# Attention projections of three head pairs as seven block products, interleaved with the retention projections

## The reference, cut to what matters

```python
h = rms_norm(x, norm1_g)
proj = h @ w_in            # 2048 x 7168: retention q, k, v, gate and attention q, k, v, 8 heads of 128 each
ret = silu(rg) * head_group_norm(retention(rotary(rq), rotary(rk), rv))
att = chunk_attention(rms_norm(aq), rms_norm(ak), av, rel_bias)
x = x + concat(ret, att) @ w_out
h = rms_norm(x, norm2_g)
x = x + square(relu(h @ w_ff1)) @ w_ff2
```

## Time and profile before

| | |
|---|---|
| median of three runs | 1105.76 us |
| the profiled execution's own time | 1104.85 us |
| its span, first to last instruction | 1103.1 us |
| granted TensorE clock | 1.000 of full speed |
| TensorE busy | 1097.7 us, 5190 records |
| VectorE busy | 857.8 us |
| ScalarE busy | 695.4 us |
| GpSimd busy | 53.4 us |
| moved by DMA | 263.81 MB, mean 239 GB/s |

### The profile page before, as it was taken

One profiled execution on the slowest core, in us unless ns is written; L12 is line 12 of the kernel. 1 busy time (PEld: TensorE's weight loads), 2 busy tenths in 40 slices (PEclk: granted clock), 3 DMA queues, 4 the chain that ended last, 5 costly groups with the idle time before them and its releaser, 6 DMA issues.

```text
span 1103.1 us, 13129 instructions
## 1 busy us (share of the span) xinstructions
PE 1097.7 (100%) x5190; PEld 932.3 (85%) x5190; DVE 857.8 (78%) x803; ACT 695.4 (63%) x827; POOL 53.4 (5%) x69
## 2 busy tenths in 40 slices
PE   9999999999999999999999999999999999999998
PEld 9789989989988888888888888888888888888887
DVE  7876876866866678869778879778869787869784
ACT  6964664674674555777655677655677655577662
POOL 0100100100100000000000000000000000000000
DMA  9975774775776647878788787797787787787792
GB/s 360 306 255 173 206 254 170 198 263 173 191 277 217 242 178 198 263 264 239 226 297 229 252 282 218 233 299 221 254 284 214 243 290 222 261 277 221 245 279 93
DMA packets 43965, 263.81 MB, mean 239 GB/s; under 512 B 4864, under 2 KB 7680, under 8 KB 16256
## 3 DMA queue, kind: packets, MB, share of 16 engines
q1 hardware_dynamic: 37712, 220.61, 53.7%
q0 software_dynamic: 5760, 41.95, 20.3%
q10 hardware_dynamic: 432, 0.41, 0.1%
HBM read 260.85 MB, written 2.10 MB: 238 GB/s over the span
## 4 chain that ended last, share of the span: by engine, by line
PE 95%; ACT 0%; DVE 0%; issue 0%; DVEq 0%
PE acc L931 10%; PE acc L927 10%; PE acc L929 10%; PE acc L797 7%; PE acc L810 7%; PE acc L804 7%; PE bankC L889 4%; PE acc L889 4%; PE bankC L882 4%; PE acc L882 4%; PE acc L884 4%; PE bankC L884 4%; PE acc L624 2%; PE acc L629 2%; PE acc L636 2%; PE bankD L889 1%
## 5 line engine op out<-in xcount | busy, mean ns | idle before, releaser
L1779 DVE TENSOR_TENSOR w_lo<-raw,w_hi 128x2048 fp32r<-128x2048 f32 x180 | 410.8, 2288 | 126.8 <-ACT w_hi L1300 126.5
L1300 ACT ACTIVATE w_hi<-raw 128x2048 fp32r<-128x2048 f32 x180 | 344.7, 1916 | 220.0 <-PE acc L931 146.6
L1497 DVE TENSOR_TENSOR w_lo<-raw,w_hi 128x1024 fp32r<-128x1024 f32 (+1 forms) x150 | 164.9, 1110 | 47.5 <-ACT w_hi L1053 47.4
L1053 ACT ACTIVATE w_hi<-raw 128x1024 fp32r<-128x1024 f32 (+1 forms) x150 | 140.6, 965 | 21.6 <-DVE raw L1506 12.6
L797 PE MATMUL acc<-w_hi,hT_hi 128*128 128x384 f32 (+1 forms) x408 | 104.3, 374 | 0.1
L927 PE MATMUL acc<-w_hi,hF_hi 128*128 128x512 f32 x256 | 100.8, 394 | 0.0
L931 PE MATMUL acc<-w_hi,hF_lo 128*128 128x512 f32 x256 | 99.7, 390 | 0.0
L929 PE MATMUL acc<-w_lo,hF_hi 128*128 128x512 f32 x256 | 99.6, 389 | 0.0
L804 PE MATMUL acc<-w_hi,hT_lo 128*128 128x384 f32 (+1 forms) x408 | 97.7, 357 | 0.0
L810 PE MATMUL acc<-w_lo,hT_hi 128*128 128x384 f32 (+1 forms) x408 | 97.2, 356 | 0.0
L927 PE MATMUL acc<-w_hi,dF_hi 128*128 128x512 f32 x248 | 96.9, 391 | 0.0
(11 more groups left out here) (276 smaller groups left out, 1798.9 us busy)
## 6 DMA issues: line engine op xcount, KB each, us to landing
raw<-in_w_up SPq DMA_DIRECT2D x64, 1024.0 KB, 6.5
raw<-in_w_down SPq DMA_DIRECT2D x64, 1024.0 KB, 6.5
raw<-in_w_ret SPq DMA_DIRECT2D x32, 1024.0 KB, 5.7
raw<-in_w_att SPq DMA_DIRECT2D x28, 768.0 KB, 4.5
raw<-in_w_out SPq DMA_DIRECT2D x16, 1024.0 KB, 4.8
raw<-in_w_up POOLq DMA_DIRECT2D x16, 1024.0 KB, 8.8
raw<-in_w_down POOLq DMA_DIRECT2D x16, 1024.0 KB, 9.1
raw<-in_w_ret POOLq DMA_DIRECT2D x8, 1024.0 KB, 9.0
```

Of the source, the lines that this page charges most:

```text
L1053: nc.scalar.activation(piece(w_hi, q, 0, n), raw[:, r, half * n:(half + 1) * n], ACT.Copy).then_inc(hi_done, 1)
L1300: nc.scalar.activation(w_hi[:, ring(s)], raw[:, r, :], ACT.Copy).then_inc(slab_hi, 1)
L1497: nc.vector.tensor_tensor(piece(w_lo, q, 0, n), raw[:, IN_PLAN[i, READ_AT.get(step, step)][0], half * n:(half + 1) * n], piece(w_hi, q, 0, ...
L1779: nc.vector.tensor_tensor(w_lo[:, ring(s)], raw[:, r, :], w_hi[:, ring(s)].bitcast(f32), ALU.subtract).then_inc(slab_lo, 1)
```

## The change

In pairs 1 to 3 the attention projection too is done as seven block products over the first half of the depth, and as plain steps I2, I3, J2, J3 over the second half. The new products carry small letters: q1, p5, p6, p7, p3, q2, p4, each 12 matmuls of 384 columns, with slabs A, B, D, E. The order of the steps alternates: the products of the attention of pair i stand between the steps of the retention of pair i - 1, and its slab steps between the retention products of pair i. Pair 0 keeps its attention steps; its retention's Z and H steps fall into the next block. The lists are now one, `IN_ORDER`, of 85 steps instead of 76. The tables of `at_piece` are written anew on all engines; products are numbered n (0 for the retention of pair 0, odd n for attention, even n for retention). Retention uses the banks A and B for all heads but head 6.

```diff
+IN_ORDER = [(0, step) for step in "I0 J0 I1 J1 I2 Q1 J2 P5 I3 P6 J3 P7 P3".split()]
+IN_LOADS = [(0, name) for name in "I0 J0 I1 J1 I2 a J2 b I3 d J3".split()]
+IN_STARTS = [0]
+for _i in range(1, BLOCKS + 1):
+    _r, _here = "Z1 Q2 Z2 P4 H1 H2", "Z1 Q2 q1 Z2 P4 p5 H1 p6 H2 p7 p3 I2 q2 Q1 I3 p4 P5 J2 P6 J3 P7 P3"
+    _loads = "Z1 e A Z2 B D H1 H2 I2 E a I3 b d J2 J3" if _i < BLOCKS else "Z1 e Z2 H1 H2"
...
         def ret_banks(u):
-            return (bankA, bankB) if u % 2 else (bankC, bankD)
+            return (bankC, bankD) if u == HEADS - 2 else (bankA, bankB)
...
-                if step == "I0" and i:
-                    pe.wait_ge(acc_read_act, 8 * i - 3 + m)
-                elif step == "J0" and i:
-                    pe.wait_ge(acc_read_act, 8 * i - 1 + m)
-                elif step == "Q1" and i:
-                    pe.wait_ge(r_mix_lo, 2 * i - 1)
-                elif step == "P5":
+                n, up = in_pair(i, step), step.upper()
+                if up == "Q1" and n:
+                    pe.wait_ge(y_set, n)
+                    pe.wait_ge(w_set, n)
+                elif up == "P5":
...
-                        fresh = step in ("I0", "J0", "Q1", "P5") and t == 0
-                        wide = N if fresh else n
+                        fresh = step.upper() in ("I0", "J0", "Q1", "P5") and t == 0
+                        wide = N if fresh and i == 0 else n
...
             def ret_proj(u):
                 i, step = u // 2, "HZ"[u % 2 == 0] + "2"
-                if u % 2:
+                if u:
                     act.wait_ge(r_y, u)
                     act.wait_ge(r_gate_ok, u)
...
+            for i in range(1, BLOCKS):
+                add_b(2 * i - 1)
+                add_e(2 * i - 1)
+                ret_power(2 * i - 2)
+                mask_bias(i)
+                add_b(2 * i)
+                ret_power(2 * i - 1)
+                att_power(2 * i)
+                add_e(2 * i)
...
+                at_piece(i, 8, ret_proj, u)
+                at_piece(i, 9, ret_tanh, u)
+                at_piece(i, 12, keep_in_p5, n - 1)
+                at_piece(i, 13, ret_qT, u)
...
+                at_piece(i, 3, in_sum, n - 1, "b", "Q1")
+                at_piece(i, 9, ret_rotate, u)
+                at_piece(i, 11, ret_rotated, u)
+                at_piece(i, 11, in_sum, n - 1, "d", "P5")
+                at_piece(i, 13, ret_kT, u)
+                at_piece(i, 14, ret_decay, u)
...
+                at_piece(i, 26, ret_decay, u + 1)
+                at_piece(i, 26, in_sum, n, "b", "Q1")
+                at_piece(i, 28, ret_norm, u + 1)
+                at_piece(i, 31, in_sum, n, "d", "P5")
```

More of the change, by code:

```diff
@@ L508, in _ @@
             load_decay(1)
[L509 to L519, removed]
+            for i, name in IN_LOADS[11:]:
+                load_in(i, name)
+                if name == "D":
+                    load_bias(i)
+                elif name == "J3":
+                    load_decay(2 * i)
+                    load_decay(2 * i + 1)
             load_group(G_OUT, w_out, 0, N)
@@ L565, in ret_power, with add_second @@
                 nc.gpsimd.tensor_tensor(r_rs[:], r_ve[:], neg_half[:, 0:MT], ALU.pow).then_inc(r_rs_ok, 1)
-            def add_ret(i, into, c, k, done, count):
-                row = ((2 * i + c) * SLABS + k) * P
-                nc.gpsimd.dma_start(raw[:, IN_PLAN[i, into][0], :], w_ret[row:row + P, :],
+            def add_second(n, into, c, done):
+                table, cols = w_att if n % 2 else w_ret, SLAB_KT * pair_cols(n)
+                row = pair_row(n, c, 1)
+                nc.gpsimd.dma_start(raw[:, pair_raw(n, into)[0], 0:cols], table[row:row + P, :],
@@ L571, in add_ret, with add_b @@
                                     accum_op=ALU.add).then_inc(done, 16)
[L573 to L582, removed]
+            def add_b(n):
+                pool.wait_ge(in_summed, 2 * n + 1)
+                add_second(n, "b", 1, in_b)
@@ L624, in group @@
                             nc.tensor.matmul(acc[par][m][:, 0:n], hi[:, k, tile_cols(m)],
-                                             piece(w_hi, j, t * n, (t + 1) * n), start=j == 0 and t == 0, stop=False)
+                                             piece(w_hi, q, t * n, (t + 1) * n), start=j == 0 and t == 0, stop=False)
                     for m in range(MT):
@@ L713, in stationary @@
             def stationary(step, m, t):
+                step = step.upper()
                 if step in ("P5", "P6", "P7", "P3"):
@@ L846, in _ @@
                     f()
-            work = {j: work.get(8 * G_OUT + j, []) for j in range(PIECES)}
+            work = {j: work.get(IN_PIECES + j, []) for j in range(PIECES)}
             work[2] = work[2] + [lambda: pe.wait_ge(a_mix_lo, HEADS)]
@@ L1264, in _ @@
-            for q in range(8 * G_OUT):
+            at_piece(0, 12, keep_in_q1, 0)
+            at_piece(0, 16, keep_in_p5, 0)
+            at_piece(0, 18, att_proj, 0)
+            at_piece(0, 20, att_squares, 0)
+            at_piece(0, 22, att_proj, 1)
+            at_piece(0, 23, att_qT, 0)
+            at_piece(0, 24, set_y, 0)
+            at_piece(0, 25, set_h, 0)
+            at_piece(0, 25, att_squares, 1)
+            at_piece(0, 26, att_exp, 0)
+            at_piece(0, 27, att_pT, 0)
@@ new lines, in _ @@
+            i, u = BLOCKS, HEADS - 2
+            at_piece(i, 6, ret_proj, u)
+            at_piece(i, 8, ret_tanh, u)
+            at_piece(i, 9, ret_qT, u)
+            at_piece(i, 12, ret_proj, u + 1)
+            at_piece(i, 12, ret_scale, u)
+            at_piece(i, 13, ret_mix, u)
+            at_piece(i, 12, ret_tanh, u + 1)
+            at_piece(i, 13, ret_qT, u + 1)
+            at_piece(i, 16, ret_scale, u + 1)
+            at_piece(i, 17, ret_mix, u + 1)
+            for q in range(IN_PIECES):
@@ L1275, in _ @@
                     f()
-            group(G_OUT, N, N, {j: work.get(8 * G_OUT + j, []) for j in range(PIECES)})
+            group(G_OUT, N, N, {j: work.get(IN_PIECES + j, []) for j in range(PIECES)})
             def hi_slab(s):
@@ L1751, in _ @@
-            for q in range(8 * G_OUT):
+            at_piece(0, 10, in_sum, 0, "b", "Q1")
+            at_piece(0, 14, in_sum, 0, "d", "P5")
+            at_piece(0, 17, x_mean_squares)
+            at_piece(0, 19, set_z, 0)
+            at_piece(0, 19, s_lo, 2)
+            at_piece(0, 20, att_mean_squares, 0)
+            at_piece(0, 21, att_norm, 0)
+            at_piece(0, 23, set_w, 0)
+            at_piece(0, 25, att_bias_max, 0)
+            at_piece(0, 26, att_probs, 0)
+            at_piece(0, 27, att_mean_squares, 1)
```

450 lines of the change are left out of this document (233 added, 217 removed).

## The result

| | before | after |
|---|---|---|
| median | 1105.79 us (4 runs, 1105.53 to 1105.92) | 1116.76 us (4 runs, 1113.22 to 1118.08) |
| the profiled execution's own time, its span | 1104.85, 1103.1 us | 1118.08, 1115.9 us |
| granted clock | 1.000 | 0.995 |

The account below looks back on a forecast made before the run. TensorE's matmul pace bounds the projection stage: profiled 1104.85 - 6.9 removed + 3.3 waits at retention scores + 2.9 at J2 = 1104.15, against the median 1105.05; forecast 1105.0 us, 8-in-10 range 1100.8 to 1109.0.

Parts of the forecast that it names:

- What the change removes: TensorE, pairs 1 to 3: 36 matmuls of 384 columns fewer (6.3 us) and narrower openings (0.65 us), 6.9 us in all.
- the openings: Opening matmuls of I0 and J0, pairs 1 to 3: twelve 512-wide ones gone, 54 ns each, 0.65 us saved.
- place A: Retention scores of a pair's first head: TensorE waits for VectorE's key copy, 1.6 us in pairs 2 and 3, together 3.3.
- in pair 1 I get 0.15: Wait at pair 1's first-head retention scores: only 0.15 us, as probabilities come two pieces later and the evacuation isn't behind them.
- place B: Slab J2, pairs 1 to 3: its load lands late beside the accumulate into b; TensorE waits 1.0 us each, 2.9 in all.
- with 8.3: J2's load assumed to take 8.3 us, from an earlier 768 KB load beside an accumulate; high part then ends at 14.3.
- The bound of 9.5: Upper bound for J2's load: landing after 9.5 us, a wait of 2.1 us a pair.
- The lower bound of this term: J2's load lands in time (4.2 us), no wait for it; VectorE's backlog before J2's first low part still leaves about 0.4.
- What moved at no price: Bank reuse, last pair's retention, GpSimd's extra transfers and other short-release slabs such as H1: costed at nothing.
- late slabs make it slower: Rival, chance 0.23: J2 takes 9.5 us, H1 lands 1 us late, TensorE waits 9.3 in all; time 1111.5 us.
- beyond about 9 us: J2 load time above which late slabs make the kernel slower, where the waits pass 9.1 us.

Follow-up runs that it names:

- the kernel with all three edits: Changed kernel with accumulate into b behind the next ret_power, first head's scores one piece later, next pair's decay loads behind Z1's load: 1103.83 us, ratio 0.9983.
- the repaired kernels: Changed kernel with the accumulate into b later (1107.02 us); also with scores one piece later, with or without decay loads moved (1103.83 us each).
- the two other kernels with such waits: Changed kernel with scores one piece later: 1111.81 us; the kernel with all three edits plus J2's load held back by one slab: 1125.55 us.

## Why the prediction was wrong

By its own steps, with the profile's spans. The parts add up: the waits at J2 +8.5, at the scores +4.8, at the first pair's P6 +1.0; TensorE's low clock +4.1 (1096.2 us busy, 1092.1 in the kernel with the accumulate moved, which has the same instructions and full clock); the removed work -5.6 (1097.7 less 1092.1). Sum 12.8, the difference of the spans.

**What the change removes: 6.9 us forecast, 5.6 measured.** The count of 36 matmuls was right, and the openings hold. The shortfall is in the steady pairs: between the attention transposes of neighbouring pairs the kernel with all three edits has 82.5 us (126.89, 209.41, 291.86), of which 0.9 are waits, so 81.6; before it was 83.5. That is 1.9 us less a pair, not 2.3. What takes the other 0.4 is open. The rows at place A show that the first two matmuls of a step behind the scores take 0.43 us (90.98 to 91.41), the next two 0.35 (91.41 to 91.76), so each restart behind a small chain product has a price. But the new order does not have more of these: in the timelines of one pair (202.99 to 286.51 before, 209.41 to 291.86 in the kernel with all three edits) there are 16 in each.

**Place A: 3.3 us forecast, 4.8 measured.** Mechanism and size were right for pairs 2 and 3 (1.6 forecast, 1.55 and 1.57 measured). The failed step is "in pair 1 I get 0.15": it measured 1.69. I had started the ledger at the probabilities' transposes, where pair 1 is ahead by an evacuation. That lead is not there when it counts: r_qk is done 0.06 us ahead of its transposes in pair 1 and 0.22 in pair 2, and from there VectorE's 5.0 us against TensorE's 3.4 are alike in all pairs. The run with the scores later shows that the wait is real: moved by one piece, 3.2 us of it go and none comes back. (The terms printed in the prediction add up to 11.6 and 10.0 where it says 11.8 and 10.1, and at place B to 13.3 where it says 13.4; nothing turns on it.)

**Place B: 2.9 us forecast, 8.5 measured.** This is the step that decided. The ledger of queues was right: from the release of J2's slot to the moment TensorE wants the slab it had 8.3 us (5.1 to 13.4), and the trace has 8.4 (115.63 to 124.00). It gave 1.0 us of wait for a load of 8.3 us, so 3.5, 2.6 and 2.7 for the 10.8, 9.9 and 10.0 us that the three loads took, and TensorE waited 3.36, 2.52 and 2.60. The failed step is the size of its load, "with 8.3". I took it from a load issued 1.5 us behind an accumulate; here it is issued 0.6 us behind, and my own ledger had 0.8 (4.3 and 5.1). Counted from the issue of the accumulate the load landed after 9.9, 9.8 and 11.0 us before, and after 11.4, 10.5 and 10.6 now. So the closer issue makes 0.9 of the 1.5 us by which the load became longer on average; the accumulates themselves take longer too (9.1, 8.9 and 10.1 before, 11.2, 10.4 and 10.5 now), and why is open. The bound of 9.5 was in my hands, and even it was too low. The experiments settle what makes the load long: with the accumulate 2.9 us behind it takes 5.7, 4.1 and 4.3 us in the three pairs, with the accumulate ahead but nearly empty 5.7, 4.5 and 4.3; put back behind the accumulate, 9.8 in all. The lower bound of this term, "still leaves about 0.4", is what the repaired kernels show, 0.40 to 0.43 us three times.

**The clock: not in the prediction at all.** The prediction put the matmuls behind a wait at the pace of full clock, without a word on it. The low clock cost 4.1 us in the profiled execution. The four runs of the changed kernel show it from the outside: clocks of 0.995, 0.995, 0.997 and 1.000 go with spans of 1115.9, 1115.5, 1113.7 and 1111.1 us. I priced a wait by its length alone; here a wait of 3.36 us cost 2.8 us more behind it (the start-to-start times of its groups of four above, each against 0.70 at full clock and 0.79 for the first), and one of 2.52 us 1.5.

**What moved at no price** held, as far as the waits show it: H1 was not late, the products' banks neither, and the waits of TensorE behind the projection stage did not change. VectorE gained 27.6 us in all (885.4 less 857.8), 9.2 a pair where I had 10.3. The rival "late slabs make it slower" was the case that came. It named the right transfer and the right threshold ("beyond about 9 us"), but paid for it with an H1 that was on time and without the clock. I gave it 0.23, because two of three loads of before had taken 8.3 and 8.4; that evidence was about a load that started later behind its accumulate.

## What to carry to other kernels

When a transfer's slack is short, look at what is issued just ahead of it on every queue: here a 3 us delay of an accumulate that nobody waited for took 9.7 us off the kernel, most of the 11.0 us by which it had been slower than the kernel before. Then look at which load now stands behind it: here it is J3, which became just as slow and could afford it. Read the load's time from a row with the same order and spacing of issues, not only the same company; counting from the issue of the transfer ahead is the safer way. And price a wait of TensorE of 2.5 us or more with the chance of a stretch at the low clock behind it, which in these kernels cost another 1.3 to 2.8 us.

## What the runs showed of the hardware

- **Who is issued first matters.** A plain load of 768 KB took 4.1 to 5.7 us when a 1 MB accumulating transfer was issued 2.9 us behind it, no more than with that transfer cut to 8 KB (4.3 to 5.7) and hardly more than alone (4.2); it took 9.8 to 11.1 us when the transfer was issued 0.6 to 0.7 us ahead, and landed 0.1 to 0.3 us after it. The accumulate took 10.3 to 11.5 us in either order. The rule that I cited (the Trainium skill, DMA: Bandwidth & Descriptors, Issuing engines are not separate DMA queues) says only that they interleave; these runs show how lopsided it can be.
- **The kind of the transfer ahead seems to matter too.** At 339.80 us of the changed kernel three plain loads of 1 MB are issued within 1 us and land after 4.9, 7.2 and 9.2 us, so one plain megabyte ahead costs about 2 us there, where the accumulating one cost J2 5 to 6. No run puts a plain megabyte ahead of J2, so this is not shown at that place.
- **The low clock behind a wait is not certain, and needs no long one.** In kernels whose other work is equal, waits of 2.52, 2.53 and 3.36 us were followed by the 1.2 GHz level, waits of 2.46, 2.60 and 3.62 us were not, and those of 5.89, 5.90 and 5.95 us were, all three. Waits up to 1.7 us at the scores and at the first pair's P6 never were. Such a stretch of matmuls lasted about 3 to 6 us and cost 1.3 to 2.8. What decides between these cases is open.
- **A kernel with such waits scatters more.** The four runs of the changed kernel lay 4.9 us apart, those of the two other kernels with such waits 1.9 and 1.6 us, those of the kernel with the accumulate moved 0.9 us.
